# The scores of the next long attention round, issued ahead of the turn of this round's weights

## The chip, the cores and the metric

The kernel runs on one core of one Trainium2 chip. The metric is the device time of one execution in microseconds, the median of several runs. A profiled execution gives a trace with the work of each engine: PE (TensorE matmuls), DVE (VectorE), ACT (ScalarE), POOL (GpSimd) and SP, which issues the DMA transfers of the weights.

## What is computed

Two transformer blocks one after the other, on 256 tokens of width 1024. The first has four branches (two attentions, a recurrence, an attention over a memory) and a feed-forward part. The second has two layers, each with a neighbourhood attention, a differential attention, a gated branch and a mixture of 16 experts. The change lies in the two attentions of these layers:

```python
def neighbourhood_attn(q, k, v, kc, vc, rpb):      # per head
    s_loc = einsum(qr, kw) * scale + bias          # 256 own keys, biased
    s_ctx = einsum(qr, kc) * scale                 # 256 context keys
    p = softmax(concatenate([s_ctx, s_loc]))
    return p_ctx @ vc + p_loc @ vw
def diff_attend(q, k, v, lam):                     # two score maps a head
    p = softmax(einsum(q, k) * dh ** -0.5)
    return (p[:, :, 0] - lam * p[:, :, 1]) @ v
```

In layer 0 the context's own 256 tokens go through both attentions too, over 256 keys only; in layer 1 they don't.

## The kernel before

Each engine has a program of its own, written by hand in a fixed order; semaphores tie them together. A core-wide `barrier` ends each stage. All weights come as one stream of 1 MB transfers into a ring of four slots. Each slot holds two pieces. For each piece ACT rounds it (L419), DVE subtracts to get the rest (L426), and PE multiplies three times (L479, L480, L481: high x high, high x low, low x high). ACT and DVE do this split three pieces ahead, at the place in their programs where they are done with an earlier piece (`next_piece`).

The attentions are written as rounds, one per pair of heads (`att_pe`, `att_act`, `att_dve`). A long round has 512 keys (`nk > T`, with T = 256); there are four in each of `na_x` (neighbourhood) and `da_x` (differential), in both layers. Short rounds have 256 keys (`na_ctx`, `da_ctx`, `mem_att`) and their scores go two rounds ahead, in banks of their own. The steps of a round r are:

- `scores(r)` on PE (L655): four matmuls of queries by keys, each of 512 columns, into PSUM banks 0 to 3. The trace shows each as two. There is one such set of banks for long rounds, so it waits until ACT has taken the exponentials of round r - 1 (`att_exp`), or in `na_x` until DVE has read the scores to add the bias (`att_read`).
- `maxima(r)` on DVE: the bias (L1732, L1733) in `na_x`, then the maximum (L785).
- `exps(r)` on ACT (L724), four of them.
- `probs(r)` on DVE: reciprocal (L790), multiplication (L794), and in `da_x` the second map times lambda (L792) added to the first (L797).
- `turn(r, j)` on PE (L670): eight transposes of the weights into banks 4 and 5. In `na_x` there are two turns a round, one for each head of the pair. It waits for `att_probs`, for ACT's copy of the turn before (`att_copied`) and until the last output is saved (`att_saved`).
- `copy(r, j)` on ACT (L739), `product(r)` on PE (L680) into bank 4, `save(r)` on ACT (L744).

Between these steps each engine does a share of other work, `also(slot)`, with banks 6 and 7. In `na_x` the slots are the query and key projections of the differential attention, each with a rotary part: PE swaps (L494), DVE multiplies and adds (L1789, L1790, L1792); the projection's bank is read by ACT (L573) in an even slot and by DVE (L574) in an odd one. A slot here is 24 matmuls. In layer 1 value projections join these slots. In `da_x` the slots are pieces of a 512-column projection in two parts: 48 matmuls a slot in layer 0, with one slot a round, and 24 in layer 1, with two a round. The bank is read after the second part, in odd slots: by ACT (L1773), and in layer 0 also by DVE (L1774). `per` is the number of slots in a round; slot 0 stands ahead of round 0.

The order on DVE is `maxima(0)`, `probs(0)`, `also(0)`, and then for each round `maxima(r + 1)`, `also`, `probs(r + 1)`, `also`. On ACT it is `copy(r, 0)`, `exps(r + 1)`, `also`, `save(r)`.

Of the kernel before, what the change touches and what calls it, by code (L numbers as in the profile page):

```python
# [224 lines left out]
def build(nc, a, out):  # L225
    ctx = ExitStack()
    with ctx:
# [383 lines left out]
        def t_of(r, nk):  # L611
            if nk == T:
                return wk((0, 1024, 4096, 5120)[r % 4], 2, 2, T)
            return wk((0, 4096)[r % 2], 2, 2, 2 * T)
# [4 lines left out]
        def scores_of(r, nk):  # L619

            if nk == T:
                return ps[:, 2 * (r % 2):2 * (r % 2) + 2, :].rearrange("p a (q k) -> p a q k", q=2)
            return ps[:, 0:4, :].rearrange("p (a q) k -> p a q k", a=2)
# [6 lines left out]
        def att_chunks(at):  # L630

            if at["diff"]:
                return [[0]]
            return [[0, 1]] if at["nk"] == 256 else [[0], [1]]
# [3 lines left out]
        def att_pe(pe, cur, at, also=lambda slot: None):  # L638
            nk, n, per = at["nk"], at["n"], at["per"]
            kc = nk // P  # L640
            base, cbase = cur.base("att"), cur.base("att_c")
            chunks = att_chunks(at)

            def scores(r):

                if at["bias"]:
                    pe.wait_ge(att_read, CREDIT + cur.base("att_b") + r - (nk == T))
                else:
                    pe.wait_ge(att_exp, CREDIT + base + r - (nk == T))
                dst = scores_of(r, nk)  # L650
                for a in range(2):
                    for qt in range(2):
                        pairs = at["qk"](r, a, qt)
                        for j, (l, m) in enumerate(pairs):
                            last = nc.tensor.matmul(dst[:, a, qt, :], l, m, start=(j == 0),  # L655
                                                    stop=(j == len(pairs) - 1))
                last.then_inc(att_scores, 1)

            def turn(r, j):
                t = t_of(r, nk)  # L660
                pe.wait_ge(att_probs, CREDIT + base + r + 1)
                pe.wait_ge(att_copied, CREDIT + cbase + r * len(chunks) + j)
                if at["y_bank"] < 6:
                    pe.wait_ge(att_saved, CREDIT + base + r)
                col = 0
                for a in chunks[j]:
                    for k in range(kc):
                        for qt in range(2):
                            b = 4 + col // 512
                            last = nc.tensor.transpose(ps[:, b, col % 512:col % 512 + P],  # L670
                                                       t[:, a, qt, k * P:(k + 1) * P], ident)
                            col += P
                last.then_inc(att_turned, 1)

            def product(r):
                pe.wait_ge(att_saved, CREDIT + base + r)
                pe.wait_ge(att_copied, CREDIT + cbase + (r + 1) * len(chunks))
                for a, rows, col, pairs in at["pv"](r):
                    for j, (l, m) in enumerate(pairs):
                        last = nc.tensor.matmul(ps[rows, at["y_bank"] + col // 512, col % 512:col % 512 + T], l, m,  # L680
                                                start=(j == 0), stop=(j == len(pairs) - 1))
                last.then_inc(att_y, 1)

            scores(0)
            if nk == T:
                scores(1)
            also(0)
            for r in range(n):
                turn(r, 0)
                if nk > T and r + 1 < n:  # L690
                    scores(r + 1)
                if per > 0:
                    also(1 + per * r)
                if len(chunks) > 1:
                    turn(r, 1)
                    if per > 1:
                        also(2 + per * r)
                product(r)
                if len(chunks) > 1 and per > 2:
                    also(3 + per * r)  # L700
                if len(chunks) == 1 and per > 1:
                    also(2 + per * r)
                if nk == T and r + 2 < n:
                    scores(r + 2)
            cur.add("att", n)
            cur.add("att_c", n * len(chunks))
            cur.add("att_b", n if at["bias"] else 0)
# [1612 lines left out]
        def _(pe):  # L2320
# [20 lines left out]
            head_norm_pe(pe, cur, mem_norm, between=lambda: v_pe(pe, cur, T))  # L2341
            barrier(pe, cur)
            att_pe(pe, cur, mem_att)
            barrier(pe, cur)
            cur.set_ring(range(6))
# [13 lines left out]
            for layer in range(LAYERS):  # L2359
# [3 lines left out]
                barrier(pe, cur)  # L2363
                cur.set_ring((6, 7))
                att_pe(pe, cur, na_x[layer], also=lambda i: (proj3_pe(pe, cur, i, n), value_pe(pe, cur, i, n) if n == T else None))
                barrier(pe, cur)
                if n > T:
                    att_pe(pe, cur, na_ctx, also=lambda i: value_pe(pe, cur, i, n))
                    barrier(pe, cur)
# [484 lines left out]
```

## Time and profile before

| | us |
|---|---|
| median of 3 runs | 3163.66 (3163.16 to 3164.96) |
| profiled execution, whole | 3157.82 |
| its span, first to last instruction | 3156.0 |
| `na_x` of layer 0, about | 1034 to 1124 |
| `da_x` of layer 0, about | 1166 to 1240 |
| `na_x` of layer 1, about | 2252 to 2365 |
| `da_x` of layer 1, about | 2365 to 2436 |

The page divides the span into 40 slices of 79 us. The two attentions of layer 0 fill slices 14 and 15 and some of slice 16, those of layer 1 slices 29 to 31. In the expert stages behind them DMA is busy throughout, at about 400 GB/s; in the attentions it moves a tenth to a third of that. The mean granted clock of PE over the whole span is 0.939 of full speed; full speed is 2.4 GHz and the other level, 0.5, is 1.2 GHz.

### The profile page before, as it was taken

What the parts mean: (1) busy time and instruction counts of PE and PEld (TensorE: products, weight loads), DVE (VectorE), ACT (ScalarE), POOL (GpSimd) and SP (SyncE); (2) the same over time, 40 slices, a digit from 0 to 9 for tenths busy, and PEclk for the clock granted to TensorE, in tenths of its full rate; (3) what the DMA queues carried; (4) which work ended last, traced back from release to release, by engine and by line L of the source; (5) the groups of instructions that cost most, each with busy time, mean ns of one, the idle gap of its engine ahead of it and who ended that gap; (6) DMA issues with size and microseconds to landing.
All of it is one profiled execution on the core that took longest, in us unless ns stands there. A gap on an engine that the chain in (4) does not pass through costs nothing. (4 is left out here: it accounts for less than half of the span.)

```text
span 3156.0 us, 37400 instructions
## 1 busy us (share of the span) xinstructions
PE 2658.4 (84%) x14844; PEld 1808.7 (57%) x14844; DVE 1170.7 (37%) x1628; ACT 871.0 (28%) x1306; POOL 40.7 (1%) x36
## 2 busy tenths in 40 slices
PE   6898999998988888799887778786896987778786
PEld 5687868798986667588652222224675973222222
DVE  4557544456744544544330011114444651000001
ACT  3455533344442333322220000003324431000001
POOL 0100000000000000000010000000000001000000
PEclk8899999999999998899979999998998997999999
DMA  4434327753542111122369999994211444999996
GB/s 155 147 133 148 107 87 273 274 200 134 181 171 78 53 56 41 41 93 102 137 254 390 404 408 406 409 395 189 76 68 62 147 147 200 408 411 413 406 413 264
DMA packets 92950, 669.42 MB, mean 212 GB/s; under 512 B 10320, under 2 KB 10496, under 8 KB 12800
## 3 DMA queue, kind: packets, MB, share of 16 engines
q1 hardware_dynamic: 90256, 654.67, 53.0%
q0 software_dynamic: 2272, 11.52, 1.0%
q8 instruction: 116, 1.90, 0.2%
q10 hardware_dynamic: 272, 1.05, 0.1%
q14 instruction: 34, 0.28, 0.0%
HBM read 666.13 MB, written 1.06 MB: 211 GB/s over the span
## 5 line engine op out<-in xcount | busy, mean ns | idle before, releaser
L2124 PE MATMUL ps<-ring,WK 128*64 128x512 f32 x3072 | 732.9, 606 | 168.4 <-DMA ring<-in_stream 144.9
L479 PE MATMUL ps<-A,piece_hi 128*128 128x256 f32 (+1 forms) x1952 | 624.7, 320 | 65.7 <-DVE A L928 19.9
L426 DVE TENSOR_TENSOR ring_lo<-ring,piece_hi 128x1024 fp32r<-128x1024 f32 x378 | 461.1, 1224 | 437.1 <-ACT piece_hi L419 436.1
L480 PE MATMUL ps<-A,piece_hi 128*128 128x256 f32 (+1 forms) x1952 | 609.9, 312 | 0.0
L481 PE MATMUL ps<-A,ring_lo 128*128 128x256 f32 (+1 forms) x1952 | 609.2, 312 | 0.0
L2124 PEld LDWEIGHTS ps<-ring,WK 128*64 128x64 f32 x3072 | 194.7, 137 | 672.8 <-DMA ring<-in_stream 371.0
L419 ACT ACTIVATE piece_hi<-ring 128x1024 fp32r<-128x1024 f32 x378 | 391.6, 1054 | 285.1 <-DVEq L505 111.8
L479 PEld LDWEIGHTS ps<-A,piece_hi 128*128 128x128 f32 x1952 | 382.4, 196 | 112.0 <-issue 74.4
L480 PEld LDWEIGHTS ps<-A,piece_hi 128*128 128x128 f32 x1952 | 383.2, 196 | 17.5
L481 PEld LDWEIGHTS ps<-A,ring_lo 128*128 128x128 f32 x1952 | 382.3, 196 | 18.2
L2244 DVE TENSOR_TENSOR WK<-WK,ps 128x512 f32<-128x512 f32 x32 | 22.0, 687 | 631.0 <-PE ps L2124 631.0
L479 PE MATMUL ps<-WKR,piece_hi 128*128 128x256 f32 (+1 forms) x624 | 188.7, 302 | 4.3 <-DVE WKR L587 2.3
L480 PE MATMUL ps<-WKR,piece_hi 128*128 128x256 f32 (+1 forms) x624 | 187.4, 300 | 0.0
L481 PE MATMUL ps<-WKR,ring_lo 128*128 128x256 f32 (+1 forms) x624 | 187.3, 300 | 0.0
L2210 ACT ACTIVATE WK<-ps 128x512 f32<-128x512 f32 x32 | 19.1, 597 | 555.7 <-PE ps L2124 555.7
L479 PE MATMUL ps<-piece_hi,A 128*128 128x256 f32 (+1 forms) x480 | 158.0, 329 | 5.1 <-DVE WK L1789 5.1
L480 PE MATMUL ps<-ring_lo,A 128*128 128x256 f32 (+1 forms) x480 | 155.0, 323 | 0.0
L481 PE MATMUL ps<-piece_hi,A 128*128 128x256 f32 (+1 forms) x480 | 154.8, 322 | 0.0
L2192 DVE COPY WK<-ps 32x512 f32<-32x512 f32 x48 | 32.7, 682 | 278.0 <-PE ps L2124 277.8
L479 PEld LDWEIGHTS ps<-WKR,piece_hi 128*128 128x128 f32 x624 | 120.0, 192 | 18.6 <-issue 14.9
L480 PEld LDWEIGHTS ps<-WKR,piece_hi 128*128 128x128 f32 x624 | 120.0, 192 | 3.7
L481 PEld LDWEIGHTS ps<-WKR,ring_lo 128*128 128x128 f32 x624 | 120.0, 192 | 3.8
(263 smaller groups left out, 2439.4 us busy)
## 6 DMA issues: line engine op xcount, KB each, us to landing
ring<-in_stream SPq DMA_DIRECT2D x621, 1024.0 KB, 7.6
WK<-in_na_bias POOLq DMA_DIRECT2D x2, 2048.0 KB, 7.9
WK<-cum_scratch POOLq DMA_DIRECT2D x1, 2048.0 KB, 9.8
const<-in_const SPq DMA_DIRECT2D x1, 1267.0 KB, 11.3
WK<-in_x SPq DMA_DIRECT2D x1, 1024.0 KB, 4.8
WK<-in_mem SPq DMA_DIRECT2D x1, 1024.0 KB, 8.5
WK<-cum_scratch POOLq DMA_DIRECT2D x1, 1024.0 KB, 16.3
WK<-in_lru_w POOLq DMA_DIRECT2D x1, 1024.0 KB, 5.6
```

The costliest lines, as they stand in the source:

```text
L419: nc.scalar.activation(piece_hi[:, no % 4, :], ring[:, slot, at:at + PIECE], ACT.Copy).then_inc(hi_done[no % 4], 1)
L426: nc.vector.tensor_tensor(ring_lo[:, slot, at:at + PIECE], ring[:, slot, at:at + PIECE], f32(piece_hi[:, no % 4, :]), ALU.subtract).then_i ...
L479: nc.tensor.matmul(out_, l[0], r[0], start=first, stop=False)
L480: nc.tensor.matmul(out_, l[0], r[1], start=False, stop=False)
L481: return nc.tensor.matmul(out_, l[1], r[0], start=False, stop=last)
L2124: last = nc.tensor.matmul(ps[64 * n:64 * n + 64, bank, :], lhs, piece[:, n * 512:n * 512 + 512], start=(k == 0), stop=(k == DC - 1))
L2192: return copy(YE[row:row + CAP, s, e // 4, half * 512:half * 512 + 512], ps[64 * half + CAP * s:64 * half + CAP * (s + 1), 6 + e % 2, :])
L2210: nc.scalar.activation(SG, ps[:, 2 * (e % 2), :], ACT.Silu).then_inc(moe_silu, 1)
L2244: nc.vector.tensor_tensor(HID[:, e % 2, :], SG, ps[:, 2 * (e % 2) + 1, :], ALU.mult).then_inc(moe_hid, 1)
```

## The change

In `att_pe`, in the loop over the rounds, `scores(r + 1)` of a long round stands ahead of `turn(r, 0)` instead of behind it. Nothing else differs. It applies to three rounds out of four in each of the four long attentions, twelve in all.

```diff
             for r in range(n):
-                turn(r, 0)
                 if nk > T and r + 1 < n:
                     scores(r + 1)
+                turn(r, 0)
                 if per > 0:
                     also(1 + per * r)
```

PE's program in `na_x` of layer 0, first round. L655 is `scores(1)`, L670 is `turn(0, 0)`, L494 the rotary swap and L479 the next projection; `att_read` and the others in brackets are the semaphores waited for:

```order
+L655 MATMUL ps<-WK 128x512 [waits att_read]
+L655 MATMUL ps<-WK 128x512 x3
 L670 MATMUL ps<-const,WK 128x128 [waits att_saved,att_copied,att_probs]
 L670 MATMUL ps<-const,WK 128x128 x7
-L655 MATMUL ps<-WK 128x512 [waits att_read]
-L655 MATMUL ps<-WK 128x512 x3
 L494 MATMUL ps<-WK,const 128x256 [waits bank_free7,bank_free6]
```

The four scores matmuls have moved over the eight of the turn; the swap and the projection now follow the turn directly.

PE's program in `da_x` of layer 0, from `product(0)` to the slot of round 1, before:

```order
L680 MATMUL ps<-WK 128x256 [waits att_copied,att_saved]
L680 MATMUL ps<-WK 128x256 x3
L670 MATMUL ps<-const,WK 128x128 [waits att_saved,att_copied,att_probs]
L670 MATMUL ps<-const,WK 128x128 x7
L655 MATMUL ps<-WK 128x512 [waits att_exp]
L655 MATMUL ps<-WK 128x512 x3
L479 MATMUL ps<-piece_hi,A 128x256 [waits bank_free7,lo_done0]
```

and now:

```order
L680 MATMUL ps<-WK 128x256 [waits att_copied,att_saved]
L680 MATMUL ps<-WK 128x256 x3
L655 MATMUL ps<-WK 128x512 [waits att_exp]
L655 MATMUL ps<-WK 128x512 x3
L670 MATMUL ps<-const,WK 128x128 [waits att_saved,att_copied,att_probs]
L670 MATMUL ps<-const,WK 128x128 x7
L479 MATMUL ps<-piece_hi,A 128x256 [waits bank_free7,lo_done0]
```

The scores of round 2 follow the product of round 0, and the turn of round 1 comes behind them. The programs of DVE, ACT, POOL and SP are the same as before, row for row.

## Rows read from the trace of the kernel before

**Rows 1.** The page, busy time of each engine with its share of the span

```profile
PE 2658.4 (84%) x14844; PEld 1808.7 (57%) x14844; DVE 1170.7 (37%) x1628; ACT 871.0 (28%) x1306; POOL 40.7 (1%) x36
```

**Rows 2.** Waits of PE, 1034 to 1240 us: waiter, releaser, total, times, longest

```profile
PE ps L670 <- DVE WK L797: 15.6, 4, 4.2
PE ps L670 <- DVE WK L794: 9.3, 3, 5.7
```

**Rows 3.** Waits of PE, 2231 to 2436 us

```profile
PE ps L670 <- DVE WK L797: 18.9, 4, 6.3
PE ps L670 <- DVE WK L794: 8.7, 1, 8.7
```

**Rows 4.** Timeline, `na_x` layer 0, first round: start, duration, operation [idle before, releaser]

```profile
1050.33 1.97 PE L670 MATMUL ps<-const,WK 128*128 128x128 f32 x8 [5.70 <-DVE WK L794]
1052.23 3.79 PE L655 MATMUL ps<-WK 64*128 64x512 f32 x8
...
1056.08 1.22 DVE L1732 TENSOR_TENSOR WK<-ps,WK 128x1024 f32<-128x1024 f32 x1 [4.67 <-PE ps L655]
...
1062.17 1.03 PE L670 MATMUL ps<-const,WK 128*128 128x128 f32 x8
```

**Rows 5.** Timeline, `na_x` layer 0, start of the second round

```profile
1072.76 1.06 PE L670 MATMUL ps<-const,WK 128*128 128x128 f32 x8 [0.57 <-ACT WK L744]
1073.75 1.99 PE L655 MATMUL ps<-WK 64*128 64x512 f32 x8
```

**Rows 6.** Timeline, `da_x` layer 0, the turns and what DVE does between

```profile
1178.92 1.69 PE L670 MATMUL ps<-const,WK 128*128 128x128 f32 x8 [3.46 <-DVE WK L797]
...
1183.63 2.29 DVE L785 TENSOR_REDUCE small<-ps 128x4 f32<-128x2048 f32 x1 [3.63 <-PE ps L655]
...
1189.66 0.69 DVE L1774 COPY WK<-ps 128x512 f32<-128x512 f32 x1 [3.74 <-PE ps L481]
...
1195.47 1.21 PE L670 MATMUL ps<-const,WK 128*128 128x128 f32 x8 [4.23 <-DVE WK L797]
...
1200.20 2.29 DVE L785 TENSOR_REDUCE small<-ps 128x4 f32<-128x2048 f32 x1 [4.78 <-PE ps L655]
...
1211.50 1.97 PE L670 MATMUL ps<-const,WK 128*128 128x128 f32 x8 [3.69 <-DVE WK L797]
...
1228.96 1.97 PE L670 MATMUL ps<-const,WK 128*128 128x128 f32 x8 [4.24 <-DVE WK L797]
...
1237.86 1.89 PE L680 MATMUL ps<-WK 128*128 128x256 f32 x8
```

**Rows 7.** Timeline, `na_x` layer 1, first round and a wait of the second

```profile
2265.91 1.97 PE L670 MATMUL ps<-const,WK 128*128 128x128 f32 x8 [8.69 <-DVE WK L794]
...
2271.66 1.22 DVE L1732 TENSOR_TENSOR WK<-ps,WK 128x1024 f32<-128x1024 f32 x1 [4.67 <-PE ps L655]
...
2278.24 1.14 PE L494 MATMUL ps<-WK,const 128*128 128x256 f32 x2 [2.27 <-DVE WK L574]
...
2283.28 2.86 PE L680 MATMUL ps<-WK 128*64 128x256 f32 x16
...
2300.79 0.70 PE L494 MATMUL ps<-WK,const 128*128 128x256 f32 x2 [1.38 <-ACT WK L573]
```

**Rows 8.** Timeline, `da_x` layer 1, the turns of rounds 0, 1 and 3

```profile
2376.37 1.97 PE L670 MATMUL ps<-const,WK 128*128 128x128 f32 x8 [6.33 <-DVE WK L797]
...
2381.53 2.29 DVE L785 TENSOR_REDUCE small<-ps 128x4 f32<-128x2048 f32 x1 [4.09 <-PE ps L655]
...
2393.19 1.22 DVE L426 TENSOR_TENSOR ring_lo<-ring,piece_hi 128x1024 fp32r<-128x1024 f32 x1
2393.32 1.09 PE L670 MATMUL ps<-const,WK 128*128 128x128 f32 x8 [4.19 <-DVE WK L797]
...
2427.15 1.97 PE L670 MATMUL ps<-const,WK 128*128 128x128 f32 x8 [4.20 <-DVE WK L797]
```

**Rows 9.** PE in a slice of 2 us: stretch, busy, clock, DMA share, GB/s

```profile
2278.00:2280.00 2.00, 1.76 (x6) 0.59 0.36 111
```

## The prediction

> **What bounds the kernel now.** I read the page first: PE is busy for 84% of the span, DVE for 37%, ACT for 28% [rows 1]. So PE sets the time almost everywhere, and a change to its order can bring no more than the stretches in which it stands idle. Next the waits of PE in the two stretches that hold the touched code, the attentions of layer 0 and of layer 1: `turn` (L670) waits for the weights that DVE makes, 15.6 us behind the last addition of the differential attention (L797) and 9.3 us behind the multiplication of the neighbourhood attention (L794) in layer 0 [rows 2], and 18.9 and 8.7 us in layer 1 [rows 3]. That is 52.5 us in 12 waits. Two of the 12, 9.3 - 5.7 = 3.6 us together, lie in the context attention, whose rounds the moved lines don't reach, and two, of 4.24 and 4.20 us [rows 6, 8], are those of the last round of each `da_x`, where no scores are left. 40.5 us in 8 waits remain. The timelines of the rounds [rows 4 to 8] then show what stands around each wait.
>
> **One long round.** PE does `turn`, `scores` of the next round, one or more projections that have nothing to do with the attention, `product`. DVE takes the maxima of those scores, ACT the exponentials, DVE the weights, and `turn` of the next round waits for them. `scores` stands behind a wait that it doesn't need: it reads only queries and keys and overwrites a bank that was read long before. With `scores` ahead of `turn`, it runs in the wait, and DVE, which is idle too (4.67 us before L1732 [rows 4]), starts the next maxima at once.
>
> Can the moved matmuls wait longer than `turn` did? No. They wait for the exponentials (or DVE's read) of round r, and `turn(r)` waits for weights made from those. Twelve `scores` move (three in each of four attentions). None is added, DVE, ACT, POOL and SP keep their order, no DMA issue is passed. What stands behind `scores` and now starts up to its length later is `turn`, ACT's copy (L739) and, in ACT's queue, the exponentials behind the copy.
>
> **`na_x`, layer 0.** First round: `turn` starts at 1050.33 after 5.70 us of idleness, `scores` at 1052.23 takes 3.79 us, and the second `turn` follows at 1062.17 [rows 4]. Warm scores take 1.99 us [rows 5]; the rest of the 3.79 is the clock, which had fallen to 1.2 GHz in the wait. If the slow stretch moves whole onto rope and projection, 1.99 us is gained, if it goes, 3.79. The nearest row is a `turn` with a projection right behind it, in the last round of `da_x` (below), which loses 1.84 us to the slow clock where this one loses 2.7: I take 2.8. Rounds 2 and 3 are PE-bound, apart from 0.57 us in which `turn` waits until ACT has saved the previous output [rows 5]. `scores` covers that: 2 x 0.57 = 1.1. If ACT's later copy cost something it would show here; the copy is needed only after a projection of almost 6 us, so I take nothing.
>
> **`da_x`, layer 0.** `turn(0)` stays where it is, at 1178.92 [rows 6]: its weights don't depend on the moved scores. From there a round now lasts until turn and projection are through and DVE, which reads the projection's bank (L1774) ahead of the weights, has made the weights. Warm turn 1.03 (the second one in [rows 4]), projection 1189.66 - 1183.63 = 6.03, from L1774 to the next `turn` 1195.47 - 1189.66 = 5.81: 12.87 us. Product (1.89) and scores (1.99) fit into the 5.81. Rounds with an even slot have no such read; there the chain of maxima, exponentials, split and weights is what ends last, 1211.50 - 1200.20 = 11.30, and it starts at `turn` itself, since DVE finds the scores ready. PE needs 1.03 + 6.03 + 1.89 + 1.99 = 10.94 in it. So turn(0) to turn(3) takes 12.87 + 11.30 + 12.87 = 37.0 instead of 1228.96 - 1178.92 = 50.0: 13.0 us. The last round keeps its wait.
>
> **`na_x`, layer 1.** First round: DVE's maxima (L1732) start at 2271.66, and they could start when the split that begins with `turn` is done, 2265.91 + 1.2 = 2267.1; the rope at 2278.24 waits for this chain [rows 7]. That is 4.6 us. Behind the 2.27 us wait, rope and projection take 2283.28 - 2278.24 = 5.04 us at a low clock; with the wait gone, between 0 and 1.5 of it goes too: 1.0. In the next round the rope's wait of 1.38 (for ACT, behind the exponentials) shrinks by the 1.0 that `turn` no longer stands ahead of `scores`. The third round gains nothing: DVE is held there by a split, not by the scores. Together 6.6 (bounds 4.6 to 8).
>
> **`da_x`, layer 1.** Two half-length projections per round. The next maxima start when the split at 2393.19, which begins 0.13 us before `turn`, is over: turn + 1.09. From the maxima to the next `turn` is 2393.32 - 2381.53 = 11.79. A round is 12.88, three are 38.6, against 2427.15 - 2376.37 = 50.8 now [rows 8]: 12.1 us. PE needs 1.03 + 6.0 + 1.89 + 1.99 = 10.9 in each, so about 2 us of idleness are left.
>
> **What the clock takes back.** The rounds of `da_x` keep waits of 0.4 to 2 us ahead of `turn`. Whether the clock falls in such a wait the rows leave open: after 1.38 us the rope took a warm 0.70, after 2.27 us it took 1.14 [rows 7], with a granted clock of 0.59 in the slice that follows [rows 9]. Its price is read from `turn` and projection with no scores between them: 1237.86 - 1228.96 = 8.90 against 1.03 + 6.03, so 1.84 us [rows 6]. I take 1.0 for all of them together; the bounds are 0 and 6.9 (rival 1).
>
> Sum: 2.8 + 1.1 + 13.0 + 6.6 + 12.1 - 1.0 = **34.6 us**. The profiled execution took 3157.82 us, 1.8 more than its span of 3156.0; less 34.6 this is 3123.2. The median of the runs lies 5.84 above the profiled one, so I forecast 3129.1. Later stages are only shifted: the expert stages wait for DMA, but the ring holds four slots, so its transfers can't run ahead into the time saved.
>
> **The rivals.** Rival 1, the clock falls in every wait that is left. In layer 0 this costs the two 12.87 us rounds 1.84 each and the middle one 1.84 - 0.36 = 1.5; in layer 1, with 2.0 of room, nothing to 0.7; and the 1.0 of `na_x` in layer 1 is lost. 34.6 + 1.0 - 5.2 - 0.7 - 1.0 = 28.7: 3135. For it speaks the 2.27 us wait, against it that these waits are shorter and PE is denser around them. [...]
>
> Rival 2, DVE and ACT don't get ahead: something in their own queues, the copy behind the later `turn` or a split that waits for a piece, holds the maxima or the exponentials where they are. Then only the scores' own time leaves the path: 8 x 1.99 + 1.1 = 17, so 3146.6. For it speaks the third round of `na_x` in layer 1. Against it: in `da_x` DVE is idle for over 3.6 us ahead of L785 [rows 6], and the maxima take 2.29 us from the start of `turn`, while the copy waits for no more than `turn` itself (1.03).
>
> Rival 3, slower: the slow clock lands on the projections and stays. The scores absorbed the slow stretch behind each wait; now the projection does. If PE ran whole `da_x` rounds at 1.2 GHz, a round would need 2 x 10.9 = 21.8 us against the 16.7 and 16.9 of now: (5.1 + 4.9) x 3 = 30 lost, less the 9.5 of `na_x`, so 3184. It decides from the point where x in 10.9 + x/2 = 16.7 is reached, when 11.6 of 16.7 us are slow. Against it: in the rows the clock is back within one `turn` and projection (the 1.84).
>
> Rival 4, nothing to see: the gain is given back, for instance by the DMA-bound stages. I see no row for that.
>
> **How the numbers follow.** Forecast 0.66, rival 1 0.17, rival 2 0.09, rival 3 0.03, rival 4 0.05. A measurement of this kernel can tell about 0.2% (6 us) from no change. The forecast spans 3126 to 3134 (a gain of 38.0 with a first `na_x` round of 3.8, 8 in layer 1 and no loss to the clock; of 29.3 with 2.0, 4.6 and half of rival 1's loss), rival 1 reaches to about 3137. The range is 3120 to 3140: with a few us for runs that differ, it holds forecast and rival 1. All 40.5 us of those waits would give 3123. Faster: 0.66 + 0.17 + 0.09 = 0.92; same 0.05; slower 0.03.
>
> **What would show it.** In the profile after: `turn` of `da_x` behind DVE at intervals near 12.9, 11.3, 12.9 (layer 0) and 12.9 three times (layer 1), with L655 ahead of it in about 2.0 us and L785 starting within about 1.3 us of `turn`; no 0.57 us wait in rounds 2 and 3 of `na_x`; the first `na_x` waits down to about 3.7 and 6.7. Intervals near 15 to 16 would mean rival 2; a turn near 1.97 and projections of 7.4 in the same rounds, rival 1. The forecast is wrong if the last waits of the long rounds keep their old length.

## The result

| | before | after |
|---|---|---|
| median, runs of the first comparison (4 and 4), us | 3163.41 (3162.10 to 3164.96) | 3119.73 (3113.08 to 3123.90) |
| ratio, 95% interval | | 0.986 (0.9841 to 0.9879) |
| profiled execution, us | 3157.82 | 3123.90 |
| its span, us | 3156.0 | 3122.1 |

The changed kernel is faster, by 43.7 us in the medians of this comparison and by 33.9 us between the two profiled executions. The forecast was 34.6 us, 3129.1, with a range that ended at 3120.0. The median fell 0.3 us below it.

The page of the changed kernel, beside [rows 1]: PE's busy time is 13.4 us shorter for the same 14844 matmuls, and DVE and ACT have the busy times they had.

```profile
PE 2645.0 (85%) x14844; PEld 1806.9 (58%) x14844; DVE 1170.4 (37%) x1628; ACT 871.2 (28%) x1306; POOL 40.7 (1%) x36
```

PE by stage, from the first scores of each long attention to the start of its last product: stretch, its length, busy PE (matmuls), granted clock, DMA share, GB/s. The kernel before, in the order `na_x` layer 0, `da_x` layer 0, `na_x` layer 1, `da_x` layer 1:

```profile
1035.32:1120.81 85.49, 77.68 (x354) 0.94 0.14 50
...
1166.11:1237.86 71.75, 56.14 (x328) 0.84 0.08 30
...
2252.16:2361.61 109.45, 91.95 (x546) 0.91 0.16 57
...
2364.98:2433.12 68.14, 49.22 (x281) 0.82 0.19 66
```

The same four of the changed kernel:

```profile
1042.52:1124.23 81.71, 76.96 (x355) 0.94 0.14 52
...
1169.46:1228.27 58.81, 50.75 (x329) 0.91 0.11 37
...
2240.23:2342.55 102.32, 89.82 (x547) 0.93 0.17 61
...
2345.91:2402.15 56.24, 45.88 (x280) 0.88 0.23 78
```

The four stages took 334.8 us and take 299.1: 3.8, 12.9, 7.1 and 11.9 us less, 35.8 in sum. The rest of the span, where the programs are the same, took 2821.2 us and takes 2823.0. So in the profiles all of the gain, and 1.8 us more, lies in the four stages. A part of it is PE's own speed: its busy time in the four is 275.0 us before and 263.4 after, 11.6 us less for the same work, and the granted clock is higher in three of them and equal in the fourth. The other 24.2 us are idle time that is gone. What makes 43.7 us of it in the medians is the subject of the first experiments.

The waits of PE in layer 0 of the changed kernel, 1034 to 1240 us (waiter, releaser, total, times, longest), answer to [rows 2]:

```profile
PE ps L670 <- DVE WK L797: 8.1, 3, 4.2
PE ps L670 <- DVE WK L794: 7.4, 3, 3.8
```

15.6 us behind L797 have become 8.1, and 9.3 behind L794 have become 7.4. The rounds of `da_x` show why, beside [rows 6] (start, duration, operation, idle before and its releaser):

```profile
1178.99 1.99 PE L655 MATMUL ps<-WK 64*128 64x512 f32 x8
...
1182.50 1.09 PE L670 MATMUL ps<-const,WK 128*128 128x128 f32 x8 [1.52 <-DVE WK L797]
...
1183.50 2.28 DVE L785 TENSOR_REDUCE small<-ps 128x4 f32<-128x2048 f32 x1
...
1191.00 1.99 PE L655 MATMUL ps<-WK 64*128 64x512 f32 x8
...
1195.30 1.09 PE L670 MATMUL ps<-const,WK 128*128 128x128 f32 x8 [2.31 <-DVE WK L797]
...
1203.48 1.89 PE L680 MATMUL ps<-WK 128*128 128x256 f32 x8
...
1205.31 1.99 PE L655 MATMUL ps<-WK 64*128 64x512 f32 x8
...
1207.23 1.09 PE L670 MATMUL ps<-const,WK 128*128 128x128 f32 x8
...
1220.04 1.46 PE L670 MATMUL ps<-const,WK 128*128 128x128 f32 x8 [4.23 <-DVE WK L797]
```

In these rounds `scores` runs ahead of each `turn` but the last, in 1.99 us each time, the time that it has at the full clock [rows 5]. DVE's maximum (L785) starts 1.00 us after `turn`, with no idle time in front of it, where in the kernel before it started 4.7 us after `turn` and had stood idle for 3.63. The turns follow each other after 12.80, 11.93 and 12.81 us, where they took 16.55, 16.03 and 17.46.

### The profile page after: what moved, and what is told of

Read it like the earlier page. It is cut to its first block and busy times, and to the rows that moved or that the text cites. A ratio compares the mean times of both kernels' runs of the same rounds, so it can differ in the third digit from the quotient of the medians.

```text
span 3122.1 us, 37400 instructions
## 1 busy us (share of the span) xinstructions
PE 2645.0 (85%) x14844; PEld 1806.9 (58%) x14844; DVE 1170.4 (37%) x1628; ACT 871.2 (28%) x1306; POOL 40.7 (1%) x36
## 5 line engine op out<-in xcount | busy, mean ns | idle before, releaser
L479 PE MATMUL ps<-A,piece_hi 128*128 128x256 f32 (+1 forms) x1952 | 626.6, 321 | 65.9 <-DVE A L928 19.9
L479 PEld LDWEIGHTS ps<-A,piece_hi 128*128 128x128 f32 x1952 | 382.3, 196 | 113.3 <-issue 75.4
L479 PE MATMUL ps<-WKR,piece_hi 128*128 128x256 f32 (+1 forms) x624 | 188.8, 303 | 5.2 <-DVE ring_lo L426 2.9
L479 PE MATMUL ps<-piece_hi,A 128*128 128x256 f32 (+1 forms) x480 | 158.9, 331 | 5.2 <-DVE WK L1789 5.2
L479 PEld LDWEIGHTS ps<-WKR,piece_hi 128*128 128x128 f32 x624 | 119.5, 191 | 19.5 <-issue 15.8
```

What stands on the lines that cost most here:

```text
L479: nc.tensor.matmul(out_, l[0], r[0], start=first, stop=False)
```

## Experiments

### Is the excess of 8 us the change's? Two controls, and each half of the change alone

Theory A says that the change gains 36 us in the four stages and nothing elsewhere. Theory B says that it also shortens the other stages. `control_before` and `control_after` are the two kernels unchanged, run again side by side. `only_da` and `only_na` move the scores in one kind of attention:

```diff
             for r in range(n):
-                if nk > T and r + 1 < n:
+                early = at["diff"]        # only_na: not at["diff"]
+                if nk > T and r + 1 < n and early:
                     scores(r + 1)
                 turn(r, 0)
+                if nk > T and r + 1 < n and not early:
+                    scores(r + 1)
```

> The kernel before, unchanged, for a second profile beside those that follow. Theory A (the change gains 36 us inside the four long attentions and nothing elsewhere; what the median shows beyond that, 8 us, is how the other stages differ from run to run): the four attentions take 85.5, 71.8, 109.5 and 68.1 us from the first scores to the last product, as in the first profile, within 1 us each, and the rest of the span moves by several us between two profiles of the same kernel. Theory B (the change also shortens other stages by about 8 us): the rest of the span is the same in both profiles of this kernel, within 2 us.

> The changed kernel, unchanged, for a second profile. Theory A: the four attentions take 81.7, 58.8, 102.3 and 56.2 us again, 35.8 less in sum; the rest of the span is that of the kernel before within its own spread, and the gain over the kernel before lies anywhere from 34 to 46 us, by the job. Theory B: the rest of the span is about 8 us shorter than in the control of the kernel before, and the gain is 42 to 46 us.

> Scores ahead of the turn in the differential attention alone (both layers). Theory A: 13.0 + 12.0 = 25 us inside the two differential attentions, the neighbourhood attentions as before (85.5 and 109.5), 25 us less in all, plus or minus 5 by the other stages. Theory B: 25 us and a share of the 8, so about 31.

> Scores ahead of the turn in the neighbourhood attention alone (both layers). Theory A: 3.8 + 7.1 = 11 us inside the two neighbourhood attentions, the differential ones as before (71.8 and 68.1), 11 us less in all, plus or minus 5. Theory B: about 13 us.

| | runs | median, us | ratio to before | four stages, us | rest of the span, us |
|---|---|---|---|---|---|
| before, these comparisons | 23 | 3164.75 (3155.64 to 3175.27) | | | |
| control_before | 12 | 3163.65 (3154.49 to 3175.65) | 1.0001 (0.9988 to 1.0013) | 335.5 | 2838.4 |
| control_after | 6 | 3127.30 (3120.13 to 3134.26) | 0.9887 (0.9868 to 0.9906) | 298.2 | 2826.9 |
| only_da | 6 | 3130.22 (3117.88 to 3147.10) | 0.9913 (0.989 to 0.9936) | 308.6 | 2807.5 |
| only_na | 12 | 3154.97 (3146.99 to 3166.37) | 0.9969 (0.9955 to 0.9984) | 324.6 | 2824.0 |

The four stages together agree within 0.9 us for the same code: 334.8 and 335.5 before, 299.1 and 298.2 after. (One of them, `da_x` of layer 1, differs by 1.2: 56.24 and 55.06.) The halves add up too, 26.2 + 10.2 us. The rest moves by 17 us between the two profiles of the one kernel before, and by 31 between `control_before` and `only_da`, whose programs don't differ there. So the first half of theory A holds: 36 us are gained in the four stages. Theory B's premise, that the rest is the same within 2 us in two profiles of one kernel, falls, and with it the possibility of reading 8 us off one pair of profiles. The medians of the halves don't decide it either: `only_da` gained 28 us by its ratio (interval 20 to 35) where A asked for 25 and B for 31, and `only_na` 10 (5 to 14) where A asked for 11 and B for 13.

The gain of the whole change in this comparison is 37.5 us by medians and 35.8 by the ratio (0.0113 x 3164.75), with an interval of 30 to 42. The four runs of before in the first comparison, within 3 us of each other, were closer together than this kernel's runs are: the next 23 spread over 20 us. All ten runs of the changed kernel, of both comparisons, have a mean of 3123.7 us, and the 39 of the kernel before that stand beside them (`control_before` with them) 3164.7. That is 41 us, about 5 more than the stages show, with an interval of 36 to 46 worked out from the spread of these runs. The second half of theory A, nothing gained elsewhere, is therefore not shown.

Where the rest's 31 us come from can be seen, if not why. The stretch between the attentions and the stretch after them, in `control_before`:

```profile
1244.11:2261.34 1017.23, 851.72 (x3783) 0.94 0.64 256
...
2442.90:3173.86 730.96, 575.28 (x2910) 0.95 0.76 305
```

and in `only_da`:

```profile
1222.72:2226.45 1003.73, 839.60 (x3783) 0.96 0.64 259
...
2394.34:3116.10 721.76, 569.64 (x2910) 0.96 0.76 309
```

In the stretch between the attentions the same 3783 matmuls keep PE busy for 12.1 us longer at a granted clock of 0.94 than at 0.96, and the stretch is 13.5 us longer. In the last stretch it is 5.6 us of busy time and 9.2 in all. What makes the clock fall more often in one execution than in the next was not tried.

### Do the scores stand on the path? The scores computed twice

`twice_before` and `twice_after` compute each of the moved scores (and no others) twice over, with the same values, in the order of before and in the new one.

```diff
-                for a in range(2):
+                for a in (0, 1, 0, 1) if nk > T and r > 0 else (0, 1):
```

> The order of the kernel before, with each of the moved scores computed twice over (the second pass overwrites the first with the same values), about 2.0 us more matmul work at each of the twelve places. Theory C (scores behind the turn stand on the path of every long round): 12 x 2.0 = 24 us more inside the four long attentions, 334.8 to about 359. Theory D (the gain of the change came from the clock, which short waits keep up, and not from where the scores stand): the extra work fills no wait here either, so 24 too; the two part in the next run.

> The changed order, with each of the moved scores computed twice over, 2.0 us more at each of the twelve places. Theory C (ahead of the turn they run in its wait): nothing in the first rounds of the neighbourhood attention, whose waits are 3.8 and 6.1 us, and 0 to 0.8 us in each long round of the differential attention with a wait of 2.3 us, about 2 in its middle round of layer 0 (no wait left there), 2.0 in the four later rounds of the neighbourhood attention, where PE has no wait: about 12 us more, 299 to 311. Theory D: 24 us more, 323.

Length of the four stages in us, and the medians of the runs (that of the kernel before is from the 15 runs beside these; the changed kernel wasn't run again beside them):

| | `na_x` 0 | `da_x` 0 | `na_x` 1 | `da_x` 1 | sum | median | ratio to before |
|---|---|---|---|---|---|---|---|
| before | 85.49 | 71.75 | 109.45 | 68.14 | 334.8 | 3160.03 | |
| twice_before | 90.97 | 77.33 | 113.01 | 74.23 | 355.5 | 3167.22 | 1.0018 (1.0006 to 1.0031) |
| changed | 81.71 | 58.81 | 102.32 | 56.24 | 299.1 | | |
| twice_after | 82.59 | 60.11 | 105.41 | 55.06 | 303.2 | 3125.38 | 0.9879 (0.9856 to 0.9901) |

Behind the turn the extra work costs 20.7 us in the stages, near the 24 that theories C and D both expect, and nearer to 12 x 1.82 = 21.8, since a second pass took 1.82 us (3.81 against 1.99) and not 2.0. Ahead of the turn the same work costs 4.1. Theory D falls: it asked for 24 there too. Theory C stands, though it asked for 12. The miss has three parts in the trace. `da_x` of layer 1 is 1.2 us shorter than in the first profile of the changed kernel, which it also is in `control_after`, without any added work. The middle round of `da_x` in layer 0 is 12.25 us instead of 11.93, not 2 us longer: the clock didn't fall behind the wait ahead of it, which was 0.50 us instead of 2.31. The largest part is the first wait of `na_x` in layer 0. There the second `turn` follows the first after 9.73 us in the changed kernel (1057.49 to 1067.22). With 1.8 us more of scores in the wait it follows after 6.85, for the same transposes, swap and projection. The changed kernel:

```profile
1051.73 1.99 PE L655 MATMUL ps<-WK 64*128 64x512 f32 x8
...
1057.49 1.97 PE L670 MATMUL ps<-const,WK 128*128 128x128 f32 x8 [3.77 <-DVE WK L794]
...
1067.22 1.04 PE L670 MATMUL ps<-const,WK 128*128 128x128 f32 x8
```

`twice_after`:

```profile
1042.77 3.81 PE L655 MATMUL ps<-WK 64*128 64x512 f32 x16
1048.60 1.09 PE L670 MATMUL ps<-const,WK 128*128 128x128 f32 x8 [2.03 <-DVE WK L794]
```

After 3.77 us of idleness the eight transposes take 1.97 us at a granted clock of 0.50 (the slice from 1057 to 1059), the 1.2 GHz level, and after 2.03 us they take 1.09 at 1.00 (1048 to 1050).

The runs tell something else than the stages here. `twice_before` is 20.7 us longer in the four stages, but its ten runs are only 7.2 us longer by the medians and 5.7 by the ratio (interval 2 to 10). In its profile the rest of the span took 2804.4 us, less than in any other (2807.5 to 2838.4). The mean granted clock of its runs was 0.941 to 0.946, that of the 15 runs of the kernel before beside them 0.935 to 0.940. So stretches whose program is the same ran some 15 us faster when work was added inside the four stages, beyond what chance gives, and no run here shows why. The comparison by stages isn't touched by this. But it is a second reason not to take for shown that the change does nothing outside the four.

### The clock by itself: more work in the first wait

`warm_first` is the faster kernel of the next section with the scores of the second round of each `na_x` computed three times over.

```diff
-                for a in range(2):
+                for a in (0, 1) * (3 if at["bias"] and nk > T and r == 1 else 1):
```

> The kernel weights_first, with the scores of the second round of each neighbourhood attention computed three times over, 3.6 us of matmuls more in the first wait (3.8 us in layer 0, 6.1 in layer 1). Theory C with the clock (a wait lets PE's clock fall to 1.2 GHz, and turn and projection behind it pay for that): from the first turn to the second in layer 0, 9.7 us become 6.8, so that attention takes 78.8 instead of 81.7, in spite of the added work; in layer 1, where 2.4 us of the wait are left and DVE's rotary chain ends last, 0 to 0.9 less. In all about 3 us less than weights_first. Rival (the slow stretch comes from something else, such as the transposes themselves): the turn stays at 1.97 us and nothing is gained, or 3.6 us are lost in each layer.

The first round in layer 0:

```profile
1046.76 5.52 PE L655 MATMUL ps<-WK 64*128 64x512 f32 x24
1052.61 1.10 PE L670 MATMUL ps<-const,WK 128*128 128x128 f32 x8 [0.33 <-DVE WK L794]
...
1059.47 1.03 PE L670 MATMUL ps<-const,WK 128*128 128x128 f32 x8
```

and in layer 1:

```profile
2244.30 1.09 PE L670 MATMUL ps<-const,WK 128*128 128x128 f32 x8 [3.25 <-DVE WK L794]
...
2251.87 0.70 PE L494 MATMUL ps<-WK,const 128*128 128x256 f32 x2 [2.30 <-DVE WK L574]
...
2256.86 2.86 PE L680 MATMUL ps<-WK 128*64 128x256 f32 x16
```

In layer 0 turn to turn took 6.86 us and the attention 78.90, against 81.72 in the kernel without the added work: 2.8 us less, as expected, for 3.5 us more of matmuls (5.52 against 1.99). The rival falls: transposes alone don't make the stretch slow. In layer 1 the expectation missed: 103.22 against 102.67, 0.6 us more where 0 to 0.9 less was expected. The turn was indeed at the full clock, although 3.25 us of idleness stood ahead of it, but being early it only made the wait ahead of the swap longer, to 2.30 us. The swap itself was still fast, 0.70, and about 1.3 us into this work the clock fell: the granted clock was 0.55 from 2253 to 2255, and swap to product took 4.99 us here and 3.50 in the changed kernel (2262.41 to 2265.91). The four stages are 281.3 us against 284.7, and the runs have a median of 3101.68, a ratio of 0.9792 (0.9767 to 0.9818) to before. Of the 3.4 us, 1.3 lie in `da_x` of layer 1 (48.10 against 49.36), whose code is the same in both; the two `na_x` together gave 2.3. That is inside the run-to-run spread, so what the added work gains is read from `na_x` of layer 0 alone and not from the runs.

### What is left of the wait: DVE makes the weights first

After the change `turn` in `da_x` waits for DVE, which reads the projection's bank and splits a piece ahead of making the weights. `weights_first` turns this around in the long rounds of `da_x`; `weights_first_old_order` does so with the scores behind the turn, as before.

```diff
+                early = nk > T and at["diff"]
                 if r + 1 < n:
                     maxima(r + 1)
-                if per > 0:
+                if per > 0 and not early:
                     also(1 + per * r)
                 if r + 1 < n:
                     probs(r + 1)
+                if per > 0 and early:
+                    also(1 + per * r)
```

> The changed order and, in the long rounds of the differential attention, DVE makes the weights of the next round ahead of reading the projection's bank and splitting a piece, instead of behind them. Theory C (what is left of a wait is DVE's chain behind the projection, 5.8 us in the odd rounds of layer 0 and maxima, exponentials, ACT's split and DVE's split, 11.8 us in layer 1): a round becomes 11.0 us, PE's own work (1.03 + 6.0 + 1.89 + 1.99), in both layers but for the split of 1.2 us in layer 1 (11.2): 58.8 to about 55 and 56.2 to about 51.5, so 8 us less than the changed kernel. Rival (the bank freed later and the split done later hold back the next projection): no gain, or up to 2 us lost in each round.

> The kernel before, scores behind the turn, with DVE making the weights ahead of reading the projection's bank and splitting a piece. Theory C (with scores on the path, a round is turn, scores at the low clock, maxima, exponentials, weights: 1.9 + 3.3 + 2.3 + 2.7 + 4.0 = 14.2 us plus 1.2 for the split in layer 1): 71.8 to about 64 and 68.1 to about 60, 16 us less than before, and still 24 us over the 284.7 of weights_first. Rival (DVE's order alone does what weights_first does): 51 and 49, as there.

| | `na_x` 0 | `da_x` 0 | `na_x` 1 | `da_x` 1 | sum | median | ratio to before |
|---|---|---|---|---|---|---|---|
| weights_first | 81.72 | 50.95 | 102.67 | 49.36 | 284.7 | 3107.69 | 0.9828 (0.9811 to 0.9846) |
| weights_first_old_order | 85.45 | 58.07 | 109.43 | 54.19 | 307.1 | 3137.60 | 0.9902 (0.9874 to 0.9930) |

`da_x` of layer 0 in `weights_first` (L1777 is before's L1774):

```profile
1175.49 1.09 PE L670 MATMUL ps<-const,WK 128*128 128x128 f32 x8 [1.54 <-DVE WK L797]
...
1184.00 1.99 PE L655 MATMUL ps<-WK 64*128 64x512 f32 x8
1184.43 1.22 DVE L797 TENSOR_TENSOR WK<-WK 128x1024 f32<-128x1024 f32 x1
1185.57 0.68 DVE L1777 COPY WK<-ps 128x512 f32<-128x512 f32 x1
1185.93 1.09 PE L670 MATMUL ps<-const,WK 128*128 128x128 f32 x8
...
1196.52 1.09 PE L670 MATMUL ps<-const,WK 128*128 128x128 f32 x8
...
1206.73 1.09 PE L670 MATMUL ps<-const,WK 128*128 128x128 f32 x8 [1.64 <-DVE WK L797]
```

The weights are there (1185.65) before the scores are through, and `turn` waits for nothing: the first two rounds take 10.44 and 10.59 us and are PE's own. The third, 10.21 us, has no scores but a wait of 1.64, where it was 4.23. That is 14.4 us off the four stages, not 8: the three rounds gave 11.7 us in both layers together, and the turn and projection behind the last wait, which the expectation left out, 3.0 more by a higher clock (6.68 us to the product instead of 8.23 in layer 0, 5.06 instead of 6.50 in layer 1). The version is faster than both kernels: its runs are 49 to 60 us below the kernel before, those of `control_after` 30 to 42 and those of the first comparison 38 to 50. The rival, that a bank freed later holds back the projection, falls.

Without the moved scores the same DVE order brings 27.7 us instead of the 16 expected. Two rounds out of three have `turn` at 1.09 us and scores at 1.99, where 1.9 and 3.3 were assumed, and take 12.3 us instead of 14.2; and behind the last wait, 1.6 us instead of 4.2, turn and projection gave 2.2 us in each layer. Its rival falls as well: the kernel stays 22.4 us behind `weights_first`. In the two `da_x` stages the moved scores bring 24.8 us alone, DVE's order 27.6 alone, and both together 39.6: each shortens the same wait, so the two gains don't add up.

## Why the prediction was right inside and wrong at its end

**The bound.** That PE's waits for the weights are what `scores` can fill was right. `twice_before` against `twice_after` shows it apart from any reading of waits.

**No longer wait.** The rule that the moved matmuls can't wait longer than `turn` did holds in all twelve places. The step "overwrites a bank that was read long before" fails in one of them: in the first round of `da_x` in layer 1 `scores` waits 2.3 us for the exponentials. The `turn` behind it still starts when the weights come, 11.39 us after the stage's first scores, as before.

**`na_x`, layer 0:** 3.9 us forecast, 3.8 measured. The first round gave 2.1 instead of 2.8, near the lower bound of 1.99: 9.73 us from turn to turn, with the slow stretch now on turn, swap and projection. The two PE-bound rounds gave 0.8 each, not 0.57 (19.50 to 18.70).

**`da_x`, layer 0:** 13.0 forecast, 12.9 measured. The rounds of 12.87 took 12.80 and 12.81. The round of 11.30 took 11.93. There `turn` still ran in 1.09 us behind the 2.31 us wait, but then the clock fell: `turn` and projection took 8.18 us up to the product instead of 6.69, and PE, not DVE, ended last. These 0.6 us were made up for by the last round, whose turn and projection took 8.23 us to the product instead of 8.90. PE in slices of 2 us from 1196:

```profile
1196.00:1198.00 2.00, 2.00 (x15) 0.68 0.00 0
1198.00:1200.00 2.00, 2.00 (x11) 0.50 0.00 0
1200.00:1202.00 2.00, 2.00 (x18) 0.96 0.00 0
```

This is rival 1, in one of the three rounds for which it asked here.

**`na_x`, layer 1:** 6.6 forecast, 7.1 measured; the first round gave 6.3 from turn to product (17.37 to 11.07), since the second slow stretch went altogether: swap to product took 3.50 us instead of 5.04, 1.5 less where 1.0 was taken.

**`da_x`, layer 1:** 12.1 forecast, 11.9 measured; three rounds of 12.78 instead of 12.88. The low clock of scores and turn in the first round cost nothing, and that of the last one 0.5 us: turn and projection took 6.50 us to the product instead of 5.97. In `control_after` they took 5.33, which is why its stage was 1.2 us shorter, 55.06.

**What the clock takes back:** 1.0 forecast, within 0 to 6.9. The sum without it was 35.6, and 35.8 was measured: what the clock took in the middle round of layer 0 (0.6), in the last one of layer 1 (0.5) and in the first round of `na_x` (0.7 against the 2.8) was made up for by the last round of layer 0 (0.7), the second slow stretch of `na_x` (0.5 beyond the 1.0) and the two PE-bound rounds. That they cancel so closely is luck. Rival 2 (17 us), rival 3 (a loss) and rival 4 didn't come true; in particular DVE did start ahead, 1.0 us after `turn`.

**The step that failed** is the last one, from the gain to the range: "with a few us for runs that differ", with the later stages "only shifted", which is a term of nothing for 2820 us of unchanged program. With it the range ended at 3120.0, and the four runs of the first comparison had a median of 3119.73. In place of a few us, the runs showed a rest of the span that moves by 17 us between two profiles of the kernel before, two medians of the changed kernel 7.6 us apart (3119.73 and 3127.30, the second inside the range), and in `twice_before` some 15 us less in stretches whose program is the same.

The 5.84 us that were added for the distance of the median from the profiled execution did no harm. To add them is to take the 34.6 off the median before, 3163.66, and in later comparisons that median was 3164.75, 3165.49 and 3160.03. It was the profiled execution, 3157.82, that was a fast one of its kernel, and that of the changed kernel lay 4.2 us above its median. Without the 5.84 the forecast would have been 3123.2, nearer to the first median of the changed kernel and farther from the second.

Not settled is whether the first comparison's 43.7 has a part that isn't chance. Its interval for the gain, 38 to 50 us, and the second's, 30 to 42, overlap; the stages give 35.8 and 37.2 for the two pairs of profiles. The stretches between the attentions and after them are shorter in both pairs, by 5.3 and 8.9 us together, but each of these differences is smaller than the same stretch's spread over the profiles.

## What to carry to other kernels

Issue first, on an engine that works in order, the work whose inputs are ready, above all ahead of a wait for a chain that this work itself feeds: in a pipeline of rounds its time then leaves the loop, and what follows it starts earlier too. Count the chain of each round from the rows, name what ends last after the move, and look whether that engine has ready work ahead of the chain as well. Read the result from the stages that changed; a difference of a few us over 3 ms needs far more runs than three.

## What the runs showed of the chip

A wait of PE costs its own length and, when the clock falls in it or behind it, the slow work that follows: 2.9 us behind the first wait of `na_x` in layer 0 (9.73 us from turn to turn against 6.85). So 3.5 us of useless matmuls in a wait of 3.8 us made this attention 2.8 us shorter. In layer 1 the same addition made it 0.6 longer, because the clock fell behind a wait of 2.30 us further on.

Waits of 2.0 to 3.3 us ended either way in these traces: 2.03 and 3.25 us with a turn of 1.09 and fast work behind it, 2.30 and 2.31 with a projection that became slow. Even the same wait of the same program did, in `da_x` of layer 1, in the profile of the changed kernel and in that of `control_after`:

```profile
2382.86 1.09 PE L670 MATMUL ps<-const,WK 128*128 128x128 f32 x8 [2.29 <-DVE WK L797]
...
2381.19 1.97 PE L670 MATMUL ps<-const,WK 128*128 128x128 f32 x8 [2.30 <-DVE WK L797]
```

The Trainium skill tells in "TensorE: Matmul & The Clock Gate", section "HAM oscillation — how this bites in real kernels", of an array that waits for a DMA of about 3 to 5 us in every pass and starts each pass at the half rate. The trace agrees for the waits of that length ahead of the turns of `da_x`: the two of 4.23 us in the changed kernel were both followed by slow work. It doesn't agree for the 3.25 us in `warm_first`, which a fast turn followed. Of the shorter ones there, 1.52, 2.31, 0.81, 0.76 and 2.29 us, only the one of 2.31 was followed by a fall of the clock, and the one of 0.81 stood behind scores that were slow already.

The same program differs by 20 us and more from one execution to the next: the kernel before took 3153.4 to 3175.7 us. The mean granted clock of the profiles ran from 0.934 to 0.949.
